# Weight slots of the expert stage: filling four of them without waiting for the first gathered block

## The reference

```
for g in range(N_GROUPS):
    a = jnp.einsum('nd,edf->nef', x, w_gate[g])
    u = jnp.einsum('nd,edf->nef', x, w_up[g])
    hh = jax.nn.silu(a) * u * gate[:, g, :, None].astype(x.dtype)
    y = y + jnp.einsum('nef,efd->nd', hh, w_down[g])
```

## Time and profile before

| what | value |
|---|---|
| median of three runs | 1191.45 us (1190.26 to 1193.11) |
| the profiled execution | 1195.13 us |
| its span, first to last instruction | 1192.9 us |
| mean granted TensorE clock | 0.946 |
| PE busy | 1053.7 us, 88% of the span |
| read from and written to DRAM | 268.66 and 28.70 MB |
| DMA queue of the weights (q1) | 238.17 MB, 53.5% of 16 engines' span |
| DMA queue of POOL's transfers (q0) | 33.88 MB, 8.6% |

### The profile page before, as it was taken

One profiled execution on the slowest core, in us unless ns is written; L12 is line 12 of the kernel. 1 busy time (PEld: TensorE's weight loads), 2 busy tenths in 40 slices (PEclk: granted clock), 3 DMA queues, 4 the chain that ended last, 5 costly groups with the idle time before them and its releaser, 6 DMA issues.

```text
span 1192.9 us, 17994 instructions
## 1 busy us (share of the span) xinstructions
PE 1053.7 (88%) x6864; PEld 747.4 (63%) x6864; DVE 416.6 (35%) x1354; ACT 232.0 (19%) x717; POOL 282.4 (24%) x445
## 2 busy tenths in 40 slices
PE   7999999969999888939999999999997999989860
PEld 6777778955555445528677686777884555545530
DVE  1134454343232222241243423435553333322226
ACT  3334441010000000023122332323301000000001
POOL 2512231021322212122111221221202232222214
PEclk9999999979999889959999999999997999989995
DMA  9312043559999999983321302154177999999985
GB/s 309 103 42 107 2 177 140 191 192 388 373 387 372 385 389 379 394 298 109 116 73 54 99 29 90 63 200 173 65 259 288 379 375 386 373 379 403 382 316 223
DMA packets 82167, 282.16 MB, mean 237 GB/s; under 512 B 10102, under 2 KB 36806, under 8 KB 64352
## 3 DMA queue, kind: packets, MB, share of 16 engines
q1 hardware_dynamic: 65216, 238.17, 53.5%
q0 software_dynamic: 15616, 33.88, 8.6%
q10 hardware_dynamic: 1248, 8.91, 1.9%
HBM read 268.66 MB, written 28.70 MB: 249 GB/s over the span
## 4 chain that ended last, share of the span: by engine, by line
PE 72%; DMA 15%; SPq 4%; DVE 4%; issue 2%; ACT 2%; POOL 1%; POOLq 0%; ACTq 0%; DVEq 0%
PE ps L1748 22%; PE ps L2042 14%; PE ps L1740 10%; DMA area<-in_w_up 9%; PE ps L2054 6%; SPq L503 3%; PE ps L2026 3%; DMA area<-in_w_down 3%; PE ps L1756 2%; PE ps L2232 2%; PE ps L1724 2%; PE ps L1801 1%; PE ps L1923 1%; PE ps L2198 1%; PE ps L1938 1%
## 5 line engine op out<-in xcount | busy, mean ns | idle before, releaser
L2042 PE MATMUL ps<-area 128*64 128x256 f32 x1040 | 255.7, 402 | 36.0 <-DMA area<-in_w_up 19.8
L1748 PE MATMUL ps<-area 128*128 128x256 f32 x1152 | 270.5, 388 | 5.6 <-ACT area L863 2.5
L1748 PEld LDWEIGHTS ps<-area 128*128 128x128 f32 x1152 | 217.0, 194 | 37.9 <-issue 5.5
L2043 PE MATMUL ps<-area 128*64 128x256 f32 x912 | 222.4, 400 | 0.0
L2042 PEld LDWEIGHTS ps<-area 128*64 128x64 f32 x1040 | 145.1, 145 | 109.5 <-issue 46.1
L664 POOL DMA_INDIRECT y_scratch<-area,idx_i x64 | 64.8, 1013 | 365.5 <-DVE area L1468 319.6
L2043 PEld LDWEIGHTS ps<-area 128*64 128x64 f32 x912 | 126.2, 144 | 0.0
L1740 PE MATMUL ps<-area 128*128 128x272 f32 x512 | 123.2, 395 | 0.0
L1453 DVE SCALAR_TENSOR_TENSOR area<-ps,area 64x256 f32<-64x256 f32 x64 | 31.4, 491 | 251.9 <-ACT area L958 251.9
L958 ACT ACTIVATE area<-ps,area 64x256 f32<-64x256 f32 x64 | 29.9, 468 | 455.1 <-PE ps L2043 455.1
L2054 PE MATMUL ps<-area 128*64 128x512 f32 x228 | 109.9, 604 | 1.1 <-DVE area L1461 0.8
(11 more groups left out here) (230 smaller groups left out, 1172.1 us busy)
## 6 DMA issues: line engine op xcount, KB each, us to landing
area<-in_w_gate SPq DMA_DIRECT2D x65, 1024.0 KB, 25.8
area<-in_w_up SPq DMA_DIRECT2D x57, 1024.0 KB, 25.6
area<-in_w_down SPq DMA_DIRECT2D x57, 1024.0 KB, 25.5
area<-in_w_b_qkv SPq DMA_DIRECT2D x12, 1024.0 KB, 6.9
hid<-in_w_up SPq DMA_DIRECT2D x8, 1024.0 KB, 26.1
hid<-in_w_down SPq DMA_DIRECT2D x8, 1024.0 KB, 25.0
area<-y_scratch ACTq DMA_DIRECT2D x8, 1024.0 KB, 7.9
area<-in_w_a_qkv SPq DMA_DIRECT2D x6, 1024.0 KB, 13.3
```

The source lines that it names most:

```text
L1748: ins = nc.tensor.matmul(ps[:r, bank, at_col:at_col + F], x[:, k, COL[t]:COL[t] + r], w[:, k, :], start=k == k0, stop=k == k1 - 1)
L2042: nc.tensor.matmul(ps[0:CAP, bank, 0:F], x[:, k, :], wg[:, k, :], start=k == 0, stop=k == KD - 1)
L2043: ins = nc.tensor.matmul(ps[CAP:P, bank, 0:F], x[:, k, :], wu[:, k, :], start=k == 0, stop=k == KD - 1)
```

## The change

The wait of SP for `gath[0]` ahead of the load to X0 is taken out, in both layers. All other waits stay, and so does the order of every queue.

```
                     for signal in free:
                         sp.wait_ge(*signal)
-                    if name == "X0":
-                        sp.wait_ge(gath[0], 16 * (NE // XG * layer + 1))
                     load(key)
```

## The result

The changed kernel takes 1197.8 us in the median (1194.78 to 1201.21, ten runs) against 1190.17 us before (1189.25 to 1193.11, ten runs): the ratio is 1.0059, 95% interval 1.0049 to 1.0069, so it is slower by 0.6%. The forecast was no change, 1191.6 us, with a range up to 1196.0; the time lies above it.

A forecast was written before the change was run, and what follows sets the result against it. The weight stream was taken to bound each expert stage's end. Earlier loads gain 1.9 + 2.6 = 4.5 us, two gather delays of 2.3 cost more: 0.1 us lost, 1191.6 us, range 1187.6 to 1196.0.

The forecast's parts named there:

- load 23: Weight load released by expert 0's down product; its data were to start 1.9 and 2.6 us earlier, less d.
- load 22: Weight load released by expert 0's gate/up; forecast to land 7 to 8 us after its issue, not 12.
- The second rival: First gather of each layer stands behind all queued weights and more: 3.1 to 5.3 us lost; chance 0.26.
- the sum: Both layers: 4.5 us from the earlier stream minus 2 d; with d = 2.3, 0.1 us lost.
- The delay d: Lateness of each layer's first gather, and so of expert 0, behind queued weights; taken as 2.3 us, bounds 0 and 3.8.
- the scaling of the gather's own rows: Gathers behind four loads lost 4.4 and 5.4 us, 0.41 to 0.5 of the queue; 0.45 x 3.8 gives 1.7 us.
- the store of layer 1: Store of rows to the scratch, 6.6 us beside one load instead of 3.7 alone; as a rule gives d 3.8 us.
- a later gather only lengthens a stretch at half clock: While PE waits before expert 0 its clock is already 0.50, so delay was to take no full-speed work away.
- The worth of the early loads: Earlier weight stream from the early start, before subtracting d: 1.9 us in layer 0, 2.6 in layer 1, 4.5 in all.
- the stream sets the end: Each expert stage's end is set by the weight stream; any shift after the stage has begun shifts the end equally.
- What was forecast to cost nothing: Last store of rows shares engines with early loads, covered by 6.3 and 5.4 us before the gather.
- the delay of less than 1 us: First rival: the gather passes between the weights by turns of queues, d = 0.7, 3.1 us gained; chance 0.18.

The follow-up runs named there:

- three early: Against the kernel before, the wait moved down so three loads per layer go out early and one is held; 1192.66 us, ratio 1.0016.
- layer 0 alone: Against the kernel before, the wait for the gather is taken out in layer 0 only; 1193.86 us, ratio 1.0026.
- gather late: Kernel with two loads early, plus ten products on POOL ahead of its first gather of each layer; 1198.77 us, ratio 1.0064.
- the gather alone: Changed kernel, but POOL issues gathers 1 to 3 only when gather 0 has landed; 1195.65 us, ratio 1.0045.
- two loads early: Against the kernel before, the wait moved down to slot H1, so two loads per layer go early and two are held; 1189.37 us, ratio 0.9986.

## Why the prediction was wrong, point by point

**The place and the sign of each mechanism were right.** The wait went, the four loads went out at once, the gather was delayed, the stream stood idle twice before load 23, and the transfers ran empty as forecast (load 22 landed 7.1 us after its issue; 7 to 8 were forecast). The second rival, the gather behind what is queued, came nearest. Two sizes were off, and both in the same direction; the sum had placed itself just where they cancelled.

**The delay d, taken as 2.3 us, measured 4.4 and 4.2 by landing.** The step that failed is the scaling of the gather's own rows. The fourth gathers of before had lost 4.4 and 5.4 us; since the queue would be shorter, I took 0.45 of what is left of it, 1.7 us, and from that 2.3 "because it is the same transfer". The queue itself was forecast well: when POOL had written the gather, 1.51 MB of weights were left, 3.9 us at 392 GB/s, where the working had 3.8. But the delay does not shrink with the queue in that way: it was 4.4 us with 1.51 MB left, and with 0.44 MB, 1.1 us, in layer 0 of three early it still was 3.5. The weights moved after POOL's write, changed kernel (255.10 to 263.50 us) and three early (255.58 to 262.00):

```profile
q1 hardware_dynamic: 345, 1.51, 46.7%
...
q1 hardware_dynamic: 72, 0.44, 18.6%
```

The rows unscaled, 4.4 and 5.4, were nearer. So was the store of layer 1, which gave 3.8, but three early doesn't bear out its rule, the whole of what is queued and no more, either. The packets show what the first gather of the changed kernel and the fourth ones of before have in common: the first packet of POOL's queue came 4.1 us after the issue in the changed kernel, and 4.4 and 4.5 us after it in the fourth gathers of before, whose queue held far more. For the one issued at 260.78, from 262.60 to 265.15 us the engines moved weights alone:

```profile
q1 hardware_dynamic: 258, 1.08, 105.3%
```

With 0.44 MB left the first packet came in time, after 1.8 us, and only the landing was late. Why the first packet waits as long as it does, and why so little weight costs 3.5 us, no run here shows.

The four loads, forecast to land 12.9 us behind the router, took 263.1 - 246.0 = 17.1. Load 17 landed 7.3 us after its issue, not the 4.9 of a lone load, since load 16 and the store were still under way (in layer 0 of the two runs in which load 16 had landed before, layer 0 alone and gather late, load 17 took 5.2 and 5.3), and the four gathers, 0.59 MB, ran among loads 19 and 20.

**Expert 0 took longer, too.** I wrote that a later gather only lengthens a stretch at half clock and takes no full-speed work away. In layer 1 the clock stayed at 0.50 (1.2 GHz) for longer after PE had begun; first before, then after, and below them PE's first transposition in both:

```profile
905.00:910.00 5.00, 5.00 (x36) 3.02 (x33) 0.06 (x1) 0.47 (x1) 0.26 (x1) 0.77 1.05 379
```

```profile
905.00:910.00 5.00, 4.16 (x24) 2.65 (x25) 0.69 (x1) 0.00 (x0) 0.93 (x1) 0.50 0.17 44
910.00:915.00 5.00, 4.69 (x28) 2.73 (x26) 1.05 (x2) 0.47 (x1) 0.00 (x0) 0.72 0.13 18
```

```profile
902.25 1.11 PE L2026 MATMUL ps<-cst,area 64*128 64x64 f32 x8 [5.25 <-DMA area<-hn_scratch,idx_i]
...
904.78 1.11 PE L2024 MATMUL ps<-cst,area 64*128 64x64 f32 x8 [9.48 <-DMA area<-hn_scratch,idx_i]
```

PE's first transposition began at 902.25 before and 904.78 after, and load 21 followed 7.2 and 8.6 us later: 1.4 us more. In layer 0 it was 7.3 and 7.5. That the longer wait of PE is the cause is not shown: with the gather alone PE waited 9.6 us in layer 1 and load 21 followed after 7.1, and with two loads early it waited 5.0 us in layer 0 and load 21 followed after 8.3. So load 21, which was to move by d, moved by 15.49 - 10.80 = 4.69 and 16.65 - 10.97 = 5.68 us: 10.4 instead of 4.6 in the two layers.

**The worth of the early loads, taken as 4.5 us, measured 2.2** (209.35 - 208.80 = 0.55 and 218.61 - 216.94 = 1.67). The working holds up to load 23: counted from load 21, it landed 1.7 us sooner in layer 0 than before (14.5 instead of 16.2 us) and 2.7 in layer 1; 1.9 and 2.6 were forecast. At the end of layer 0 a third of it is left, less than held stages differ by among themselves. In layer 1 the 1.5 us at load 25 and the 1.7 at the end agree. Where the rest goes is not settled.

**The step "the stream sets the end" was half right.** The stream is full from load 23 on, and PE waits for it at the end as before; but where a load went early, what shifts a full stream is the release of its first load that PE holds. The run with the late gather shows it at its plainest. So the sum by the measured terms is 2.2 - 10.4 = -8.2 us, the 8.15 of the traces, against 7.6 by the medians.

**What was forecast to cost nothing did cost nothing.** Between the last router product and the gather's issue there were 253.98 - 246.0 = 8.0 us after and 256.85 - 248.87 = 8.0 before, with full transfers beside it now, and the store was in time.

The Trainium skill ("DMA: Bandwidth & Descriptors", Queues, rings and completion order) has a transfer engine take turns between its queues a packet at a time. The traces agree only from the gather's first packet on, when packets of both queues lie in one stretch (76 and 80 from 258.30 to 260.60 us with the gather alone); they show no turns in the 2.65 us before, and the delay of less than 1 us that I worked out by that rule did not come. The same section says that the count by which a transfer is known to have landed is written only after every earlier write of that engine, across its queues. That is no more than a small part of the delay here: with the gather alone its last packet had started by 260.60, and the landing came 0.5 us later.

## What to carry to other kernels

An idle stretch of the transfers ahead of a bound stage is worth at most what the first load that the consumer still holds gains by it; find that load and count from its release. If the start of the consumer hangs on a small transfer, let ahead of it only what is all but through when that transfer's data start (here two of four loads): weights left in the queue cost the small transfer 2.0 to 4.4 us here, not in proportion to their bytes. When a sum comes out as the difference of two uncertain terms of equal size, the nearest measured row decides it, and a row scaled by a proportion that no row shows is no measured row.

## What the runs showed of the hardware that was not expected

The time from PE's first transposition to the granted clock's return from 0.50 to 1.00 was not fixed: 5.2 and 5.0 us before, 5.7 and 8.0 in the changed kernel, and between 4.9 and 7.8 in the other runs without throwaway products in which it was read, also in stages where the gather came at the same time behind the same wait; layer 1 of the run with the wait taken out in layer 0 alone, the same stage as before, has 5.9. Load 21, which waits for the first expert's gate and up, followed that transposition after 7.1 to 8.6 us in these stages, so 1.5 us of a first expert is left to it. With throwaway products in PE's wait the clock was back before the first transposition, and load 21 followed after 5.6 to 5.7 us; eleven of them took 5.8 to 7.2 us, more than the wait they were to fill.

A gather issued by POOL into a full stream of weights moved nothing for its first 3.8 to 4.5 us, twice as long as alone (1.75 and 1.9 us), whether 1.1 MB of weights were left behind it or the four loads of before and more.
